# Last tiles of each sum by token halves, and norms over both halves before either is scaled, in a two-block transformer on one core

## The reference

```python
for l in range(DEPTH):                      # DEPTH = 2
    h = _rmsnorm(x, pre_mix_norm[l])
    h = _hybrid_mixer(h, cos, sin, w_in[l], ..., w_out[l])       # ends in mixed @ w_out
    x = x + _rmsnorm(h, post_mix_norm[l])
    h = _rmsnorm(x, pre_ffn_norm[l])
    h = _conv_glu_ffn(h, ffn_up[l], ffn_conv[l], ffn_conv_bias[l], ffn_down[l])
    x = x + _rmsnorm(h, post_ffn_norm[l])

def _conv_glu_ffn(h, ffn_up, ffn_conv, ffn_conv_bias, ffn_down):
    u = _causal_dwconv(h @ ffn_up, ffn_conv) + ffn_conv_bias
    gate, val = jnp.split(u, 2, axis=-1)
    return (jax.nn.gelu(gate, approximate=True) * val) @ ffn_down
```

## Time and profile before

| | before |
|---|---|
| median of 3 runs | 1241.99 us (1241.88 to 1242.41) |
| the profiled execution: own time / span | 1241.33 us / 1239.5 us |
| PE busy, share of the span | 1168.0 us, 94% |
| DVE busy | 831.3 us, 67% |
| ACT busy | 674.8 us, 54% |
| POOL busy | 133.2 us, 11% |
| mean granted clock of PE | 0.956 of full speed |

### The profile page before, as it was taken

The page is one execution under the profiler, slowest core; times in us unless marked ns, Lnnn a source line. Parts: engine busy times, 40 slices in busy tenths (PEclk is TensorE's granted clock), DMA queues, the critical chain, the costliest instruction groups (busy, mean ns, idle before and its releaser), DMA issues.

```text
span 1239.5 us, 21178 instructions
## 1 busy us (share of the span) xinstructions
PE 1168.0 (94%) x7776; PEld 1061.2 (86%) x7776; DVE 831.3 (67%) x1357; ACT 674.8 (54%) x1142; POOL 133.2 (11%) x169
## 2 busy tenths in 40 slices
PE   8999899899999899979989999988896899899998
PEld 8998788899999799968889999988896688788886
DVE  6756555777777695565467777775964557557995
ACT  6654245655555676423556555566731445546784
POOL 0002500000000000161000000003882000000000
PEclk9999999999999899999989999999996588999999
DMA  7543003366666364410136656543331015667992
GB/s 244 184 146 111 36 1 118 112 188 189 183 186 186 90 198 142 146 41 1 55 102 199 183 185 187 185 153 111 112 120 51 1 35 187 250 178 255 354 347 93
DMA packets 49799, 181.10 MB, mean 146 GB/s; under 512 B 5568, under 2 KB 5728, under 8 KB 49600
## 3 DMA queue, kind: packets, MB, share of 16 engines
q1 hardware_dynamic: 48816, 176.98, 44.3%
q0 software_dynamic: 912, 3.16, 0.7%
HBM read 179.07 MB, written 1.05 MB: 145 GB/s over the span
## 4 chain that ended last, share of the span: by engine, by line
PE 83%; DVE 7%; POOL 4%; ACT 4%; issue 1%; DMA 1%; DVEq 0%; ACTq 0%; SPq 0%; POOLq 0%
PE bank L1662 22%; PE bank L1663 21%; PE bank L1664 21%; PE bank L1743 2%; PE bank L1897 2%; PE bank L1886 2%; PE bank L1895 2%; PE bank L1721 1%; PE bank L1729 1%; POOL y L2593 1%; POOL region L1605 1%; PE bank L1712 1%; POOL region L1580 1%; POOL region L1583 1%; PE bank L1749 1%
## 5 line engine op out<-in xcount | busy, mean ns | idle before, releaser
L2247 DVE TENSOR_TENSOR w<-ring,w 128x1024 fp32r<-128x1024 f32 x234 | 287.7, 1231 | 116.1 <-ACT w L2002 116.1
L1662 PE MATMUL bank<-act,w 128*128 128x256 f32 x1216 | 351.3, 289 | 11.6 <-DVE w L2247 5.7
L1663 PE MATMUL bank<-act,w 128*128 128x256 f32 x1216 | 347.0, 285 | 0.0
L1664 PE MATMUL bank<-act,w 128*128 128x256 f32 x1216 | 346.8, 285 | 0.0
L2002 ACT ACTIVATE w<-ring 128x1024 fp32r<-128x1024 f32 x234 | 246.3, 1053 | 77.0 <-PE bank L1664 74.5
L1662 PEld LDWEIGHTS bank<-act,w 128*128 128x128 f32 x1216 | 236.3, 194 | 16.3 <-issue 11.3
L1663 PEld LDWEIGHTS bank<-act,w 128*128 128x128 f32 x1216 | 236.4, 194 | 2.0
L1664 PEld LDWEIGHTS bank<-act,w 128*128 128x128 f32 x1216 | 236.1, 194 | 0.0
L2521 DVE SCALAR_TENSOR_TENSOR region<-bank,pf,region 128x255 f32<-128x255 f32 (+1 forms) x176 | 84.8, 482 | 40.5 <-ACT region L2207 29.4
L1662 PE MATMUL bank<-w,hid 128*128 128x512 f32 x214 | 85.0, 397 | 2.2 <-DVE hid L2534 2.2
L1663 PE MATMUL bank<-w,hid 128*128 128x512 f32 x214 | 84.5, 395 | 0.0
(11 more groups left out here) (412 smaller groups left out, 2184.0 us busy)
## 6 DMA issues: line engine op xcount, KB each, us to landing
ring<-wtiles SPq DMA_DIRECT2D x234, 512.0 KB, 3.6
ring<-etiles SPq DMA_DIRECT2D x33, 512.0 KB, 4.9
act_raw<-etiles SPq DMA_DIRECT2D x33, 512.0 KB, 5.1
sq<-etiles SPq DMA_DIRECT2D x22, 512.0 KB, 4.9
cst<-etiles SPq DMA_DIRECT2D x8, 512.0 KB, 5.0
region<-packp POOLq DMA_DIRECT2D x4, 512.0 KB, 4.2
cst<-consts SPq DMA_DIRECT2D x1, 1348.0 KB, 11.9
x<-xt SPq DMA_DIRECT2D x2, 512.0 KB, 5.9
```

What stands on the lines that cost most here:

```text
L1662: t.matmul(out_, still[:, 0], moving[:, 0], start=first, stop=False)
L1663: t.matmul(out_, still[:, 0], moving[:, 1], start=False, stop=False)
L1664: return t.matmul(out_, still[:, 1], moving[:, 0], start=False, stop=last)
L2247: v.tensor_tensor(w_lo[:, s, :], ring[:, s, :], w_hi[:, s, :].bitcast(F32), ALU.subtract).then_inc(lo_ready, 1)
```

## The change

It touches the four turnings and the tile steps around them.

1. **Token halves.** Of each sum's last tiles (three at the mixer's end, two at the feed-forward part's) PE does all c = 0 products first, then all c = 1 products, where before each tile did both. A tile is done, for the refills, when its c = 1 half is.
2. **Norms reordered.** DVE does gain and add for c = 0 and c = 1, and only then scales c = 0 and c = 1; before, the scaling of c = 0 stood between c = 1's gain and add.
3. **Turning by 512 columns.** The scaling is two instructions of 512 columns for each c; PE starts on each as it is there. The eight turned blocks lie in the four banks in another arrangement: both token halves of a block stand side by side in one bank, so ACT and DVE read 256 adjacent columns. `keep_warm` between the two c is 2 and not 4.
4. **Refills moved.** At the mixer's end one refill stands between c = 0 and c = 1 of the norm after, one behind the norms (ahead of `pre_hi` and `pre_lo`); both stood ahead of the norms. At the feed-forward part's end one refill goes from ahead of the norms to behind them.
5. **The last gated part.** In the last pair of the feed-forward part, DVE multiplies right behind its convolution, ahead of the refills' splits, and high and low part go to a buffer of their own (`last_hi`, `last_lo`, over `thin`), so that they need not wait for the `down` tile that still reads `hid`. The last turn of the hardware loop is written out on ACT and DVE for that.
6. **A root's table.** ACT takes one root of a constant ahead of the norm behind the feed-forward part, so that the load of that function's table comes there.

```diff
-            def token_product(banks, still, s, first, last):
-                for c in range(NT):
+            def token_product(banks, still, s, first, last, halves=range(NT)):
+                for c in halves:
                     for j in range(2):
                         mm = product(bank[banks[c] + j], still[:, :, c * P:(c + 1) * P],
                                      w_both[:, :, s, j * HALF:(j + 1) * HALF], first, last)
                         if last and 2 * c + j < 2 * NT - 1:
                             mm.then_inc(sums_done, 1)
-                mm.then_inc(tile_done, 1)
+                if NT - 1 in halves:
+                    mm.then_inc(tile_done, 1)
...
             def turn(i, banks):
                 for c in range(NT):
-                    pe.wait_ge(pre_scaled, i * NT + c + 1)
-                    for k in (*range(0, KD, 2), *range(1, KD, 2)):
-                        mm = transpose(bank[banks[k % 2] + c][:, k // 2 * P:k // 2 * P + P], scaled[:, c, k * P:(k + 1) * P])
-                        if c == NT - 1 and k >= KD - 2:
-                            mm.then_inc(pre_turned, 1)
+                    for g in range(2):
+                        pe.wait_ge(pre_scaled, (i * NT + c) * 2 + g + 1)
+                        for odd in range(2):
+                            for k in range(g * KD // 2 + odd, (g + 1) * KD // 2, 2):
+                                mm = transpose(turned(banks, k, slice(c * P, (c + 1) * P)), scaled[:, c, k * P:(k + 1) * P])
+                            if c == NT - 1:
+                                mm.then_inc(pre_turned, 1)
                     if c < NT - 1:
-                        keep_warm(4)
+                        keep_warm(2)
...
-                for i in range(2, KD):
+                for i in range(2, KD - SLOTS):
                     out_part(i)
+                for c in range(NT):
+                    for i in range(KD - SLOTS, KD):
+                        out_part(i, (c,))
                 keep_warm(14)
                 turn(2 * l + 1, LAYER_SUMS)
...
-                for p in range(NP_FF, NP_FF + DOWN_LAG):
-                    step(r0 + (NP_FF - 1), 1 + p - NP_FF, p, p % PAIRS, up=False, stop=p == NP_FF + DOWN_LAG - 1)
+                for c in range(NT):
+                    for p in range(NP_FF, NP_FF + DOWN_LAG):
+                        step(r0 + (NP_FF - 1), 1 + p - NP_FF, p, p % PAIRS, up=False, stop=p == NP_FF + DOWN_LAG - 1, halves=(c,))
...
-                for k in range(1, KD - 1):
+                for k in range(1, KD - SLOTS):
                     refill(T_WOUT + k)
-                post_root(2 * l, l * LAYER_TILES + T_UP)
+                post_root(2 * l, l * LAYER_TILES + T_UP, lambda: refill(T_UP - 3))
...
+                refill(T_UP - 2)
                 pre_hi(l * 16 + 8, lambda k: pf_("pre", k), LAYER_SUMS)
...
+                a.activation(credit[:, 19:20], eps, ACT.Sqrt)
                 post_root(2 * l + 1, (l + 1) * LAYER_TILES)
...
-                v.tensor_scalar(scaled[:, c, :], x[:, c, :], x_inv[:, c:c + 1], None, ALU.mult).then_inc(pre_scaled, 1)
+                for j in range(2):
+                    part = slice(j * HALF, (j + 1) * HALF)
+                    v.tensor_scalar(scaled[:, c, part], x[:, c, part], x_inv[:, c:c + 1], None, ALU.mult).then_inc(pre_scaled, 1)
...
                 for c in range(NT):
                     result_gain(ch, r, c, post)
-                    if c >= 1:
-                        pre_scale(i, c - 1)
                     result_add(ch, r, c)
-                pre_scale(i, NT - 1)
+                    if c == 0 and between:
+                        between()
+                for c in range(NT):
+                    pre_scale(i, c)
...
+                            if late and w == 1:
+                                hidden_part(p, q)
                             refill_lo(r, k + w)
                         k = k + 2
+                    if late:
+                        hidden_low(p, q, last_hi, last_lo)
                     if down:
                         refill_lo(r, k)
```

More of the change, by code:

```diff
@@ L2017, in pre_hi, with post_root @@
                 for k in range(KD):
-                    if k < 2:
-                        act.wait_ge(pre_turned, at // KD * 2 + k + 1)
+                    g, i = divmod(k, KD // 2)
+                    if i < 2:
+                        act.wait_ge(pre_turned, at // KD * 4 + 2 * g + i + 1)
                     else:
                         act.wait_ge(h_lo, at + k - 1)
-                    a.activation(token_rows(act_hi[:, k, :]), turned(banks, k), ACT.Copy, scale=gain(k)).then_inc(h_hi, 1)
-            def post_root(r, last):
+                    a.activation(act_hi[:, k, :], turned(banks, k), ACT.Copy, scale=gain(k)).then_inc(h_hi, 1)
+            def post_root(r, last, between=None):
                 for c in range(NT):
+                    if c == 1 and between:
+                        between()
                     for j in range(2):
@@ L2212, in step @@
                         k = k + 2
-                    if down:
+                    if down and not late:
                         refill_hi(r, k)
@@ L2223, in layer @@
                     step(r0 + (p - 1), 1, p, p % PAIRS)
-                with act.Fori(0, GLU_LOOPS) as i:
+                with act.Fori(0, GLU_LOOPS - 1) as i:
                     for q in range(PAIRS):
                         step(r0 + i * PAIRS + (q + PEEL - 1), 1, i * PAIRS + (q + PEEL), q)
-                for p in range(NP_FF, NP_FF + DOWN_LAG - 1):
-                    step(r0 + (NP_FF - 1), 1 + p - NP_FF, p, p % PAIRS, up=False)
+                for p in range(NP_FF - PAIRS, NP_FF):
+                    step(r0 + (p - 1), 1, p, p % PAIRS, late=p == NP_FF - 1)
+                a.activation(credit[:, 19:20], eps, ACT.Sqrt)
                 post_root(2 * l + 1, (l + 1) * LAYER_TILES)
@@ L2541, in layer @@
                     step(r0 + (p - 1), 1, p, p % PAIRS)
-                with dve.Fori(0, GLU_LOOPS) as i:
+                with dve.Fori(0, GLU_LOOPS - 1) as i:
                     for q in range(PAIRS):
                         step(r0 + i * PAIRS + (q + PEEL - 1), 1, i * PAIRS + (q + PEEL), q)
-                for p in range(NP_FF, NP_FF + DOWN_LAG - 1):
-                    step(r0 + (NP_FF - 1), 1 + p - NP_FF, p, p % PAIRS, up=False)
+                for p in range(NP_FF - PAIRS, NP_FF):
+                    step(r0 + (p - 1), 1, p, p % PAIRS, late=p == NP_FF - 1)
                 residual(ch, 2 * l + 1, 2 * l + 2, post_ffn)
+                refill_lo(r0 + (NP_FF - 1), 1)
                 dve.wait_ge(packa_in, l * 16 + 32)
```

67 lines of the change are left out of this document (38 added, 29 removed).

## The result

| | before | changed |
|---|---|---|
| median of 4 runs of each, us | 1241.93 (1241.86 to 1242.41) | 1222.16 (1220.55 to 1222.42) |
| ratio | | 0.9837, 95% interval 0.9820 to 0.9854 |
| profiled execution, us | 1241.33 | 1222.39 |
| its span, us | 1239.5 | 1220.6 |

The prediction was 1221.5 us with a range of 1217.5 to 1228.5. Its forecast case is the one that came, and each of its terms is found again in the profile. Their sum is two us short of what the first block gained, and some us were lost in the second block, which the prediction had not looked at; so part of the closeness is luck.

A forecast was written before the change was run, and what follows sets the result against it. The prediction took PE's matmuls to bound the kernel, so gains come at the four turnings: 3.2 + 3.2 + 5.1 + 4.6 + 4.3 (clock) = 20.4 us off 1241.33, a median of 1221.5 us; range 1217.5 to 1228.5.

The forecast's parts named there:

- What bounds: Whole kernel: matmuls bound it, PE 83% of the chain; the change acts only where the chain leaves PE.
- Token halves, M0 and M1: Turnings behind the mixers of layers 0 and 1: c = 0's norm runs beside c = 1's matmuls; each turning gains 3.2 us.
- The reordering: Norm at M0: c = 1's add no longer waits behind c = 0's square, root and scaling; starts 215.6, was 218.70.
- Turning by 512 columns: Between scaling and turn at the turnings: the turn starts 0.27 us earlier; the split before the first low part costs 0.45.
- The last gated part and the table, F0 and F1: Turnings behind the feed-forward parts, layers 0 and 1: 1.1 us of idle PE goes; gains 5.1 and 4.6 us.
- The table load off the path: Ahead of the norm behind the feed-forward part: ACT's 1.28 us load moves earlier, costing c = 0 half a us off the path.
- Rival 2: Late table: ACT stands another 1.28 us behind the added load, 1.05 us at each feed-forward turning, 1223.6 us; chance 0.06.
- The clock: At the four turnings: the granted clock holds and no longer falls to 1.2 GHz; 4.3 us more.
- rival 1: Clock still falls at the turnings: 1225.9 us if nothing comes back, 1228.5 if F1 falls too; chance 0.20.
- The start: Turning at the program's start: taken at nothing; fewer short matmuls there can save a fraction of a us.
- Rival 3: No cover at the mixer's end: a late last tile costs some 3.5 us at M0 and M1, 1228.5 us; chance 0.05.
- rival 4: Slower: the clock stays low behind the turnings, some 32 us of low clock to lose, up to 1258 us; chance 0.02.

The follow-up runs named there:

- Experiment 2: Changed kernel with the last tiles whole (both token halves of each tile) at the end of both sums: 1227.25 us, ratio 0.9895.
- experiment 7: Changed kernel with two instead of three tiles by token halves at the mixer's end: 1221.61 us, ratio 0.9836.
- experiment 1: Changed kernel with the old norm order, c = 0's scaling again between c = 1's gain and add: 1233.61 us, ratio 0.9947.
- experiment 8: Changed kernel with each token half's scaling as one instruction of 1024 columns: 1220.51 us, ratio 0.9837.
- experiment 10: Changed kernel without short matmuls at the four turnings and with one scaling of 1024 columns: 1220.2 us, ratio 0.9825.
- experiment 3: Changed kernel with the last gated part back behind the splits, in the old buffer, token halves kept: 1227.96 us, ratio 0.9899.
- experiment 4: Changed kernel without the added root of a constant, so the table load is back in the norm: 1221.44 us, ratio 0.9846.
- experiment 5: Kernel before the change with more short matmuls at the turnings (20 instead of 14, 11 instead of 4): 1234.77 us, ratio 0.9946.
- experiment 6: Changed kernel without the short matmuls at the four turnings: 1219.71 us, ratio 0.9833.
- experiment 9: Changed kernel once more, nothing edited: 1221.25 us, ratio 0.9819 to the kernel before.

## Why the prediction held, step by step

- **What bounds.** Right. PE's matmuls were as many and as long as before, and the time came from the four turnings and the feed-forward parts' ends: 21.2 of the 22.2 us that the ledger's first four rows hold.
- **Token halves, M0 and M1 (3.2 each).** Measured 3.26 each. The cover of c = 0's norm held: its add ended at 211.9, 0.6 us ahead of the last product, and the low parts of the last tiles were in time, which had been costed to fit by 0.2 us. Experiment 2 takes the cover away (2.4 us at M0; 3.2 at M1, of which 0.8 is the clock), experiment 7 a third of it (1.0).
- **The reordering.** "The whole gain of the reordering is here" is right in mechanism: the second add came 1.8 us behind the sums' end, as predicted, and 2.08 us later in experiment 1. Only, the halves and the order need each other: taking out either costs 8.0 or 7.6 of the 14.3 us of gaps. At F the add came 1.9 us behind the sums' end, where I had 2.1.
- **Turning by 512 columns (turn 0.27 earlier).** The turn started 0.55 us behind its scaling, as predicted from 0.81. The price set beside it, the split between the last scaling and the first low part, was right in kind; its size was 0.34 (the low part 0.92 behind ACT, it had been 0.58) where I had 0.45. What the prediction did not draw from it: with the split last, the earlier turn is worth nothing (experiment 8), except at a low clock (experiment 10).
- **The last gated part and the table, F0 and F1 (5.1 and 4.6).** Gap and part's end together gained 4.10 + 1.32 and 3.64 + 1.32: 5.4 and 5.0. The idle PE was 1.26 and 1.27 us by start to start, a little over the 1.10 of the row. The prediction put the old sums' end at 414.6; the last product ran from 414.30 for 0.40, so it was 414.7, which changes nothing. Taken out of the finished kernel the late part costs 4.2 us a time, not 1.1 (experiment 3): the term was rightly sized for what the change takes away from before, and would have been wrong as the worth of that part.
- **The table load off the path.** Right. The root ran 1.29 to 1.30 us behind the start of the load, here (403.81 to 405.11) as in the earlier trace rows and in experiment 4 (407.31 to 408.60). The load's drain of some 1380 ns that the Trainium skill names (page "ScalarE: Activation LUTs", section "What ACT_TABLE_LOAD costs") no run here shows. Rival 2, which rested on a load twice as long, would have put the first square some 1.2 us later than 405.21. With all else in place the moved load is worth 0.65 us at each F turning (experiment 4), half of its length.
- **The clock (4.3).** Measured 4.27, and 0.45 of F0's gap besides: the granted clock was 1.00 in every turning, with PE idle for 0.6 to 0.7 us ahead of the first turn and 0.92 behind the last. Experiment 1, with gaps 2.08 longer, had it fall at three of four; experiment 5 held it up in the kernel before. That it holds because the idle times ahead of and behind the last turn became short is only half shown: filled idle time holds it (experiment 5) and without any short matmul it fell (experiment 6), but the argument against rival 1, that every fall came with a gap of 1.9 us or more, holds for the turnings and not for the whole trace. The last section has a fall behind 7.2 us of busy PE.
- **The start (nothing).** It gained 0.99 us in the first profile and 0.47 in the second of the same kernel. The eight profiles of kernels with the changed kernel's start had their first product from 13.71 to 14.78, the two with the start of before at 14.70 and 14.99. So most of it can be a draw of the execution, and whether the fewer short matmuls there give anything is not shown.
- **What was left out: the second block.** It took 3.1 us more than in the kernel before in one execution and 1.3 in the other. The first block's terms summed to 22.2 where I had 20.4, and this loss brought the net to 18.9. That the median came within 0.7 us is in part luck: two errors of 2 and 3 us had opposite signs.

Rival 1 (the clock still falls) did not come; experiment 1 shows it for the kernel without the new order. Rival 3 (no cover) did not come, nor rival 4, whose sign would have needed 32 us of low clock.

## What to carry to other kernels

Where a chain of small steps on several engines stands between two stretches of matmuls, look for what can be done on half of the tokens while PE still works on the other half, and then let the last half's steps queue behind nothing that isn't theirs. Here the two need each other: with either missing the gaps were 6.2 or 6.7 us shorter than before, with both 14.3. Value each part by taking it out of the finished kernel too, since a part that looks worth 1.1 us may be what another stands on (4.2). Read the gap from last to first product, which came out the same to 0.05 us in two executions of the changed kernel, ahead of the whole time, which hides parts of under 2 or 3 us.

## What the runs showed of the hardware

- The low stretches of the granted clock come at places that no edit touched, and not in each kernel. Stretches of 5 us at the same work of the second mixer, in the changed kernel (115 us behind the 49th matmul of F0) and without its short matmuls:

```profile
536.61:541.61 5.00, 5.00 (x29) 4.44 (x28) 1.13 (x4) 1.19 (x2) 1.20 (x1) 0.69 0.05 18
```

```profile
538.51:543.51 5.00, 5.00 (x42) 4.55 (x41) 2.57 (x8) 2.18 (x6) 1.20 (x1) 1.00 0.05 20
```

  PE is busy for all 5.00 us in both, with 29 matmuls at 0.69 and 42 at 1.00. That mixer took about 193.1 (kernel before, changed, experiments 3, 4, 7, 8, 9) or about 191.6 (experiments 1, 5, 6, 10), and this stretch is the difference; in experiment 2 it took 194.7, and the first mixer 197.3 where all others had 198.7 to 199.0. The second block, the same code in all kernels, took from 392.71 to 396.75. The losses behind the turnings of experiments 6 and 10, 2.2 and 1.5 us, went with 1.6 less in the second mixer; but experiment 5 had 1.4 less there and lost nothing at the turnings. Why the low stretch comes in one kernel and not in another is not settled.
- A fall can come behind a busy PE: in experiment 3 the matmuls after the wait of 2.41 us started at full clock (0.39 us each), and only at 408.70 did one take 0.59, a us after PE had resumed.
- A fall can come with no wait of PE at all. In the second block of the kernel before PE was busy for all of 1018 to 1025.2 at 1.00, and the clock is 0.62 from 1024 to 1029, with PE busy throughout:

```profile
1018.00:1025.20 7.20, 7.20 (x59) 6.84 (x58) 5.18 (x9) 5.46 (x9) 0.00 (x0) 1.00 0.00 0
1024.00:1029.00 5.00, 5.00 (x29) 4.78 (x29) 3.39 (x15) 0.73 (x1) 0.00 (x0) 0.62 0.00 0
```

  So the falls at the turnings go with idle time of PE, as experiments 1, 5 and 6 show, but not every fall in this program does.
